# Differential attention: the product with the values taken with the values standing still in high and low halves, two query blocks at a time, and the stacks' low halves on GpSimd

## The reference

```
s = einsum('bqhcd,bkhcd->bhcqk', qblk, kh) * scale      # two components c per head
p = softmax(s, axis=-1)
p_diff = p[:, :, 0] - lam * p[:, :, 1]
o = einsum('bhqk,bkhv->bqhv', p_diff, vh)
o = rmsnorm(o, subln_g) * (1.0 - lam_init) * silu(g)
```

## Time and profile before

| | |
|---|---|
| median of 3 runs | 1480.43 us (1480.12 to 1480.55) |
| the profiled execution | 1481.06 us, span 1479.3 us |
| TensorE matmul busy | 1462.7 us (99%) |
| VectorE busy | 1091.1 us (74%) |
| ScalarE busy | 822.9 us (56%) |
| GpSimd busy | 106.9 us (7%) |
| the chain that ended last | TensorE 88%, VectorE 6%, ScalarE 3% |

### The profile page before, as it was taken

One profiled execution on the slowest core, in us unless ns is written; L12 is line 12 of the kernel. 1 busy time (PEld: TensorE's weight loads), 2 busy tenths in 40 slices (PEclk: granted clock), 3 DMA queues, 4 the chain that ended last, 5 costly groups with the idle time before them and its releaser, 6 DMA issues.

```text
span 1479.3 us, 27771 instructions
## 1 busy us (share of the span) xinstructions
PE 1462.7 (99%) x11060; PEld 1388.5 (94%) x11060; DVE 1091.1 (74%) x1811; ACT 822.9 (56%) x1754; POOL 106.9 (7%) x110
## 2 busy tenths in 40 slices
PE   9999999999999999999999999999999999999998
PEld 8999999999999999999999999999988889999987
DVE  6878887788665777777667778778885657777754
ACT  6565555665434655665555555656654435665554
POOL 0000110011100000000000001001011000000010
PEclk9999999999999999999999999999999999999999
DMA  5212112111223222222132121212112232222221
GB/s 195 74 63 66 58 58 68 62 58 58 72 68 93 71 73 72 73 72 72 58 101 86 58 72 60 69 58 72 58 58 81 67 112 72 72 72 86 74 85 72
DMA packets 34560, 109.92 MB, mean 74 GB/s; under 512 B 4864, under 2 KB 4992, under 8 KB 34432
## 3 DMA queue, kind: packets, MB, share of 16 engines
q1 hardware_dynamic: 34432, 108.15, 23.6%
HBM read 97.38 MB, written 2.10 MB: 67 GB/s over the span
## 4 chain that ended last, share of the span: by engine, by line
PE 88%; DVE 6%; ACT 3%; issue 2%; DMA 0%; SPq 0%; DVEq 0%; ACTq 0%
PE proj L1642 59%; PE pair L1774 5%; PE far L1889 4%; PE pair L1874 2%; PE pair L1876 2%; PE far L1903 2%; PE far L1891 1%; PE far L1760 1%; PE pair L1825 1%; PE far L1742 1%; PE far L1844 1%; PE far L1845 1%; PE far L1782 1%; PE far L1848 1%; PE pair L1832 1%
## 5 line engine op out<-in xcount | busy, mean ns | idle before, releaser
L1642 PE MATMUL proj<-u_hi,w_hi 128*128 128x264 f32 (+1 forms) x2024 | 484.8, 311 | 3.5 <-DVE w_lo L1122 2.1
L1642 PE MATMUL proj<-u_hi,w_lo 128*128 128x264 f32 (+1 forms) x2024 | 458.6, 298 | 0.0
L1642 PE MATMUL proj<-u_lo,w_hi 128*128 128x264 f32 (+1 forms) x2024 | 458.3, 298 | 0.0
L1642 PEld LDWEIGHTS proj<-u_hi,w_hi 128*128 128x128 f32 x2024 | 322.5, 189 | 16.0 <-DVE w_lo L1122 2.5
L1642 PEld LDWEIGHTS proj<-u_hi,w_lo 128*128 128x128 f32 x2024 | 321.6, 188 | 10.8
L1642 PEld LDWEIGHTS proj<-u_lo,w_hi 128*128 128x128 f32 x2024 | 321.7, 188 | 7.2
L1122 DVE TENSOR_TENSOR w_lo<-w_raw,w_hi 128x1024 fp32r<-128x1024 f32 x178 | 217.3, 1221 | 43.6 <-ACT w_hi L710 43.5
L935 ACT ACTIVATE decay<-pair,neg_max 128x528 f32<-128x528 f32 (+1 forms) x144 | 100.4, 697 | 218.2 <-DVE neg_max L1501 218.0
L710 ACT ACTIVATE w_hi<-w_raw 128x1024 fp32r<-128x1024 f32 x178 | 186.3, 1047 | 28.6 <-PE proj L1642 25.5
L1501 DVE TENSOR_REDUCE neg_max<-pair 128x1 f32<-128x528 f32 (+1 forms) x144 | 101.4, 704 | 110.5 <-PE pair L1876 110.3
L1774 PE MATMUL pair<-q_level,qk_dec 128*128 128x128 f32 x768 | 104.6, 279 | 3.6 <-ACT q_level L868 3.5
(11 more groups left out here) (237 smaller groups left out, 2353.0 us busy)
## 6 DMA issues: line engine op xcount, KB each, us to landing
w_raw<-w_units SPq DMA_DIRECT2D x178, 512.0 KB, 3.5
q_stack<-gate_f SPq DMA_DIRECT2D x32, 132.0 KB, 2.4
k_stack<-k_stack SPq DMA_DIRECT2D x32, 132.0 KB, 2.4
h<-x_t SPq DMA_DIRECT2D x8, 264.0 KB, 5.9
cos_sin<-rope SPq DMA_DIRECT2D x2, 528.0 KB, 5.7
out_t<-ops SPq DMA_DIRECT2D x2, 512.0 KB, 3.5
out_t<-decay SPq DMA_DIRECT2D x2, 512.0 KB, 3.9
masks<-level_masks SPq DMA_DIRECT2D x1, 448.0 KB, 5.7
```

Source lines behind the costliest of these rows:

```text
L1642: ins = pe.matmul(out, w, x[:, tile, cols_n], start=(k == 0 and p == 0), stop=(k == last_k and p == 2))
```

## The change

The values are now kept as a rounded high half and a low half (v_hi, v_lo, and v_meta_hi, v_meta_lo for the meta tokens) and stand still in TensorE; the turned weights are kept as p_hi and p_lo and move, two query blocks at a time (`weigh_values`), in three single-pass products. ScalarE rounds (`raise_v`, `raise_turned`), VectorE subtracts from PSUM (`cut_v`, `cut_turned`). The result comes out turned, ScalarE copies it (`take_values`), TensorE turns it back to rows (`rows_back`), and ScalarE takes the rows with their scales (`take_rows`) and squares them (`square_rows`); for the second group of layer 0 that is in the first step of the next head. `stack_low` moves from VectorE to GpSimd. In a step TensorE runs a part of the pieces ahead of the later half of the attention work and the rest behind it (`after_pieces`).

```
-AT_FEED = (3, 3, 3, 2, 2, 3, 2, 3, 2, 3, 2, 2, 2)
-LAST_FEED = (3, 3, 3, 3, 2, 2, 2, 2, 2, 2, 2, 1, 1)
+AT_FEED = (3, 3, 3, 2, 3, 2, 2, 2, 3, 3, 2, 2, 2)
+LAST_FEED = (3, 3, 3, 2, 2, 2, 2, 2, 2, 3, 2, 1, 1)
 def stack_steps(l, c):
-    last = 2 * query_chunks(l) - 1
-    return (LEVELS, TURN_KEYS + 1) if c < HG_HEADS else (last, last + 1)
+    return (LEVELS, TURN_KEYS + 1) if c < HG_HEADS else (2 * query_chunks(l) - 1, TURN_KEYS + 1)
+def turn_main_step(c):
+    return 1 if c == HG_HEADS else 2
+def after_pieces(c, s):
+    return 1 if s in (3, 10, 11, 12) else 2
 # units_followed
-    {"ak": 2 if wide else 1, "ag": 2 if wide else 3, "outA": 0, "outB": 0, "any": 2}
+    {"ak": 2, "ag": 2 if wide else 3, "outA": 0, "outB": 0, "any": 2}
 # GpSimd
+            def stack_low(a):
+                for i in range(2):
+                    for comp, rows in enumerate(comps):
+                        pool.wait_ge(stack_hi, 4 * a + 2 * i + comp + 1)
+                        low = gate_f[rows, 2, :] if i == 0 else k_low[rows, comp, :]
+                        pool.tensor_tensor(low, gate_f[rows, i, :],
+                                           (q_stack, k_stack)[i][rows, comp, :].bitcast(f32),
+                                           ALU.subtract).then_inc(stack_lo, 1)
+                        pool.wait_ge(stack_lo, 4 * a + 2 * i + comp + 1)
...
+                    if c == HG_HEADS - 1:
+                        stack_low(l * AT_HEADS)
                     if c > 0:
                         cut_mixed(n - 1)
+                    if HG_HEADS <= c < HEADS - 1:
+                        stack_low(l * AT_HEADS + c + 1 - HG_HEADS)
                     invert_rms(n)
 # ScalarE, in attend
-                if s == 1:
-                    copy_v(n)
+                if s == 0:
+                    raise_v(n)
+                    if l < LAST and c > HG_HEADS:
+                        square_rows(l, c - 1, 1)
+                if s == 6:
+                    take_values(l, a, 0)
+                if s == 2 * chunks + 2:
+                    take_values(l, a, 1)
+                if s == 8:
+                    take_rows(l, c, 0)
+                    square_rows(l, c, 0)
+                if s == 11 and l == LAST:
+                    take_rows(l, c, 1)
+                    square_rows(l, c, 1)
 # VectorE
+            def cut_turned(l, c, s):
+                a = l * AT_HEADS + c - HG_HEADS
+                chunks, chunks_before = query_chunks(l), before(a, 5, AT_HEADS)
+                j = (s - 3) // 2
+                if s % 2 == 0 or not 0 <= j < chunks:
+                    return
+                rows = P if j < 4 else N_META
+                dve.wait_ge(pt_hi, chunks_before + j + 1)
+                dve.tensor_tensor(p_lo[:, :, in_group(j)], turned_p(rows), p_hi[:, :, in_group(j)].bitcast(f32),
+                                  ALU.subtract).then_inc(pt_lo, 1)
 # TensorE
+            def weigh_values(l, c, g):
+                a = l * AT_HEADS + c - HG_HEADS
+                chunks_now = before(a, 5, AT_HEADS) + group(l, g)[-1] + 1
+                pe.wait_ge(v_lo_ready, a + 1)
+                pe.wait_ge(pt_lo, chunks_now)
+                cols_n = group_cols(l, g)
+                out = meta[:, P:P + cols_n]
+                for kk in range(4):
+                    for at, (v, p) in enumerate(((v_hi, p_hi), (v_hi, p_lo), (v_lo, p_hi))):
+                        pe.matmul(out, v[:, kk, :], p[:, kk, 0:cols_n], start=(kk == at == 0), stop=False)
+                pe.matmul(out, v_meta_hi[:, :], p_hi[:, 4, 0:cols_n], start=False, stop=False)
+                pe.matmul(out, v_meta_hi[:, :], p_lo[:, 4, 0:cols_n], start=False, stop=False)
+                pe.matmul(out, v_meta_lo[:, :], p_hi[:, 4, 0:cols_n], start=False, stop=True).then_inc(pv_done, 1)
...
+            def attend_later(l, c, s):
+                if s == 0:
+                    turn_v(l, c)
+                if s == turn_main_step(c):
+                    pe.wait_ge(v_lo_ready, a + 1)
+                    turn_main(n - 1)
+                    turn_meta(n - 1)
+                if s == 3:
+                    turn_p(l, c, 0)
+                if s == 6:
+                    weigh_values(l, c, 0)
+                if s == 8:
+                    rows_back(l, c, 0)
+                if s == 2 * query_chunks(l) + 2:
+                    weigh_values(l, c, 1)
+                if s == 11 and l == LAST:
+                    rows_back(l, c, 1)
```

More of the change, by code:

```diff
@@ L511, in squares, with group, group_cols, in_group @@
             return slice((j % N_CHUNKS) * P, (j % N_CHUNKS + 1) * P)
+        def group(l, g):
+            return range(2 * g, query_chunks(l) if g else 2)
+        def group_cols(l, g):
+            return sum(P if j < N_CHUNKS else N_META for j in group(l, g))
+        def in_group(j):
+            at = (j % 2) * P if j < N_CHUNKS else 2 * P
+            return slice(at, at + (P if j < N_CHUNKS else N_META))
+        def in_o_t(j):
+            return slice(j * P, j * P + (P if j < N_CHUNKS else N_META))
+        def turned_p(rows):
+            return far.rearrange("p a n -> p (a n)")[:, 0:5 * P].rearrange("p (k n) -> p k n", k=5)[:, :, 0:rows]
         def two(ap):
@@ new lines, in square_rows @@
+            def square_rows(l, c, g):
+                n, a = l * HEADS + c, l * AT_HEADS + c - HG_HEADS
+                last = query_chunks(l) - 1
+                for j in group(l, g):
+                    rows = P if j < 4 else N_META
+                    if j == group(l, g)[0]:
+                        act.wait_ge(act_step, own[0])
+                        act.wait_ge(o_taken if g else rows_read, n + 1 if g else a + 1)
+                    ins = act.activation(sq[0:rows, squares(j)], o_rows[0:rows, j, :], ACT.Square,
+                                         accum_out=o_sums[0:rows, j:j + 1])
+                    if j < last:
+                        step(ins)
+                    else:
+                        ins.then_inc(sq_ready, 1)
@@ L1571, in _ @@
                             finish_turn(l, i)
-                        for i in range(2):
-                            if s == low_steps(l, c)[i] and HG_HEADS <= c + 1 < HEADS:
-                                stack_low(l * AT_HEADS + c + 1 - HG_HEADS, i)
                         for i in units_taken(c, s):
@@ L1662, in last_piece, with feed @@
                 ins.then_inc(last_done if tile < EARLY_TILES - 1 else unit_done, 1)
-            def feed(l, c, s):
-                for i, k in fed_pieces(c)[pieces_by(c, s - 1):pieces_by(c, s)]:
+            def feed(l, c, s, first=0, end=None):
+                for i, k in fed_pieces(c)[pieces_by(c, s - 1):pieces_by(c, s)][first:end]:
                     piece(l, i, k)
@@ L1862, in attend @@
                 if s == 0:
+                    if l < LAST and c > HG_HEADS:
+                        rows_back(l, c - 1, 1)
                     pe.wait_ge(stacked, 16 * 4 * (a + 1))
```

225 lines of the change are left out of this document (133 added, 92 removed).

## The result

The changed kernel takes **1523.57 us** (median of 6 runs) against 1480.49 for the kernel before in the same runs: a ratio of 1.029, interval 1.0276 to 1.0298, 43 us slower. I had forecast 1496.5 with a range that ended at 1509. The direction is right, the size is not.

A forecast was written before the change was run, and what follows sets the result against it. TensorE, busy 99% of the span, was taken as a thin bound. Six steady heads per layer at +0.55 (layer 0) and +2.4 us (layer 1), -1.9 and +0.3 elsewhere, gave +16 us: 1496.5 us as a median, range 1468 to 1509.

The forecast's parts named there:

- TensorE's own work: Values product and turns back, per attention head: 1.3 to 1.4 us less in layer 0, 0.5 less in layer 1.
- The last turn: Turn of a steady head's last query block, waiting for VectorE's weights: stall of 1.2 us in layer 0, 1.0 in layer 1.
- rival 3: GpSimd's next subtraction starts ahead of VectorE's waiting one, holding qk_dec a second 1.3 us: 1511 us; chance 0.1.
- The keys' transfer: Layer 1, before the next head's scores: key stack, rounded behind the second product, lands 1.0 us late; hidden in layer 0.
- The second product in layer 1: Layer 1, behind the last turn: block 3's low half ready at 10.1, wanted at 9.5, a 0.55 us stall.
- Step 3 and the steps behind it: Scores waiting for exponentials, 0.3 us per head; later waits 0.6 in layer 0 (steps 5 to 8), 0.25 in layer 1.
- The two estimates without a row: VectorE's 640-column low half, taken as 0.82 us, and GpSimd's subtraction on 64 partitions, taken as 1.3.
- Rest: Outside steady heads: head 8 -1.4 and -0.5 us, head 15 about nothing, layer 0's last turn +0.3.

The follow-up runs named there:

- e4: The kernel before, with only the four subtractions moved to GpSimd and its product with the values unchanged: 1492.33 us.
- e5: The changed kernel with GpSimd's second subtraction alone held back until VectorE has written the last block's weights: 1504.55 us.
- e6: The changed kernel with layer 1's keys rounded at step 9 instead of 10 and the keys' transfers issued ahead of the queries': 1515.88 us.
- e3: The changed kernel with 14 unneeded transposes on TensorE ahead of its wait for the last block's weights in each attention head: 1515.44 us.
- e1: The changed kernel with GpSimd's four subtractions held back until VectorE has written the last block's weights: 1516.49 us.
- e2: The changed kernel with the four subtractions back on VectorE, the new product kept: 1516.56 us.
- e8: e7 with the turn of layer 0's last block one projection piece later: 1488.56 us.
- e7: e6 with the query stack's low half back on VectorE and the keys' left on GpSimd: 1492.57 us.
- e10: e8 with all four subtractions on GpSimd for each layer's first attention head, and the previous head's mix rounded in step 4 instead of 3: 1488.83 us.
- e11: e10 with layer 0's query subtraction on VectorE done in two pieces around p_lo: 1488.56 us.

## Why the prediction was wrong, point by point

- **TensorE's own work.** 256 columns took 0.118 us as forecast, 272 took 0.125. But the product with the values was cheaper before than I had priced it. Summed from start to start over six heads of a layer it took 5.12 us per head in layer 0 and 4.10 in layer 1, not 5.55 and 4.44: my 1.11 came from one product and counted a slow first pair of the projection behind it. In heads without a fall of the clock it takes 3.65 and 3.62 now, and the turns back 0.38 and 0.30. The gain is 1.09 and 0.18 us, not 1.35 and 0.5, some 10 us in all instead of 15.
- **The last turn (the step that failed).** My chain let GpSimd hold VectorE once there. Forecast 1.2 and 1.0 us late; measured 2.34 and 2.15 from start to start, 27 us over twelve heads instead of 13. The chain was right up to qk_dec, and then GpSimd held it a second time, 1.05 us more: rival 3 came true, to which I gave 0.1. My reason against it, that in rows 6 the held instruction was followed at once by the next, could not bear it: there GpSimd had one instruction and nothing behind it. e4 and e5 show the second hold on either kernel. The Trainium skill (SBUF — State Buffer, Who interferes with whom) states the lock in terms of who issues first; the traces agree. GpSimd's second instruction starts 0.08 us after its first ends (502.40 to 502.48), VectorE's next 0.10 after its own one before ends (502.42 to 502.52), and it is the later one that is held.
- **The clock (the term that was not there).** I had costed each stall at its own length, and the fall of the clock at nothing; it cost 11.5 us. Rival 3's 1511 plus these 11.5 is 1522.5; measured 1523.6. That it comes so close is in part luck: the gain on TensorE was 5 us smaller than in that sum, and the term for the second product, 3 us, was not there.
- **The keys' transfer.** Forecast 1.0, measured 0.81 idle and 1.08 from start to start; e6 took 1.1 per head back.
- **The second product in layer 1.** Forecast 0.55; in the change nothing. In e5, with the turn at 1.0 as I had thought, it waits 0.6: the term was right for a turn that is on time by the forecast, and the later turn of the change covered it.
- **Step 3 and the steps behind it.** Forecast 0.3 for the exponential in either layer, 0.6 for steps 5 to 8 of layer 0 and 0.25 for layer 1. The scores, from start to start, went from 4.91 to 5.55 us per head in layer 0 and from 3.94 to 4.42 in layer 1: right in size.
- **The two estimates without a row.** The low half of 640 columns was put at 0.82 us and took 0.82 (1248.27); GpSimd's subtraction was put at 1.3 and took 1.32 or 1.30.
- **Rest.** Forecast -1.6; measured -2.7.

The sum by the measured terms, per steady head: layer 0 37.9 - 1.1 + 0.6 + 2.4 = 39.8 (39.87), and 1.5 more in most for the clock; layer 1 34.8 - 0.2 + 0.5 + 2.1 + 1.0 = 38.2 (38.18).

## What to carry to other kernels

A stall can cost more than its length: a fall of TensorE's clock added 1.3 to 1.5 us here. In steady heads it came behind 11 of 12 stalls of 2.2 us, behind 6 of 24 of 1.9 to 2.15 us, and behind none of 1.6 us or less, so price the long ones with a share of it. Where such a stall cannot be removed, work that nobody needs can pay for itself (e3). Before putting two instructions with two SBUF inputs in a row on GpSimd, look at what VectorE has to do at that point: its instruction with two SBUF inputs was held by both, and one wait between them was worth 19 us. And when a wait is taken away, price the next wait on the same chain before the gain; in e1, e2 and e8 it took most of it.

## What the runs showed of the hardware

- **How long an idle time brought the clock down.** In steady heads it fell
  - after 2.16 to 2.19 us, in layer 0, five times of six in the change and six of six in e6;
  - after 1.98 to 1.99 us, in layer 1, twice of six in the change and in e6 alike;
  - after 1.9 to 2.15 us in layer 0 of e1 once of six, and after 2.0 us in layer 0 of e2 once of six.

  Outside them it fell after 2.0 us both times in e7, once of two in e8, and after 3.3 us once of two in e10 and both times in e11. It did not fall in e1's, e2's, e4's and e5's steady heads behind waits of 1.1 to 1.6 us, nor in e3 (0.8 at most). The same idle time brings it down in one head and not in the next. The fall began between 0.3 us before TensorE started again and 1.5 us after it. Each lasted 3.4 us, and twice (626 to 634 in the change, once in e6) two followed one another.
- **A wait costs 0.1 us more than the idle time shown.** TensorE in the change, at the scores behind the late exponential:

```profile
484.52 0.40 PE L1757 MATMUL proj<-u_hi,w_lo 128*128 128x264 f32 x2
485.12 0.39 PE L2038 MATMUL pair<-k_stack,q_stack 128*128 128x264 f32 x1 [0.20 <-ACT decay L1039]
485.35 0.29 PE L2040 MATMUL pair<-k_low,q_stack 128*128 128x264 f32 x1
485.47 0.28 PE L2038 MATMUL pair<-k_stack,q_stack 128*128 128x264 f32 x1
```

The scores start 0.6 us after the last pair of the projection, 0.35 more than a pair's 0.245, where the profile shows 0.20 idle, and the next matmul comes 0.23 later instead of 0.12. In that head four of ten score groups begin so, where one did before, and three of them with no idle time listed: the ends of matmuls in the profile are modelled and can cover such a wait, so the starts have to be compared.
- **GpSimd is held too.** Its subtraction on 64 partitions takes 1.3 us alone (2.70 for two with the 0.08 between them), the same as mix_lo on 128. The third of the row of four starts at 503.86, while VectorE's held weights still run (to 504.34), and takes 3.42 us. It ends at 507.28, 1.2 us after the end of w_lo:

```profile
504.88 1.20 DVE L1219 TENSOR_TENSOR w_lo<-w_raw,w_hi 128x1024 fp32r<-128x1024 f32 x1
```

  So the hold works in both directions. Why GpSimd did not go ahead between 504.34 and 504.88, where VectorE had only v_t, with one input from PSUM, is not shown.
